# Four heads and both out-projections of the first mixer in one block, the second mixer's compression inside its in-projection

## What is computed

```python
# first mixer (mLSTM, 4 heads of 512), evaluated for all 512 tokens at once
x_in, z = jnp.split(h @ w_in, 2, axis=-1)
x_conv = silu(causal_conv4(x_in)); q, k, v = blockwise 4x4 products
s = (q k^T / sqrt(512)) * weights(i, f gates), causal
hh = s @ v / max(|s.sum(-1)|, floor); hn = layernorm(hh) * ln_w
x = x + ((hn + skip * x_conv) * silu(z)) @ w_out
# second mixer (nsa_mixer), 16 query heads in 4 groups of head size 64
q, k_c, v_c, k_s, v_s, k_w, v_w, z, g_logit = split(h @ w_in)
k_cmp = silu(blocks of 32 tokens, stride 16, of k_c + pe, @ w1[0]) @ w2[0]   # v_cmp alike
p_cmp = masked_softmax(q k_cmp^T * scale)                                     # 31 columns a head
q_r, k_s, k_w = rope_partial(...)
o = gate0 * (p_cmp @ v_cmp) + gate1 * selected attention + gate2 * window attention
x = x + (o * silu(z)) @ w_out
```

## Time and profile before

| what | value |
|---|---|
| median of 3 runs | 2141.22 us (2139.99 to 2141.77) |
| the profiled execution | 2139.64 us, of which the span is 2137.9 us |
| mean granted TensorE clock | 0.946 |
| TensorE, Vector, Scalar busy | 91%, 53%, 32% of the span |
| HBM | 73 GB/s over the span |

### The profile page before, as it was taken

One profiled execution on the slowest core, in us unless ns is written; L12 is line 12 of the kernel. 1 busy time (PEld: TensorE's weight loads), 2 busy tenths in 40 slices (PEclk: granted clock), 3 DMA queues, 4 the chain that ended last, 5 costly groups with the idle time before them and its releaser, 6 DMA issues. The chain is left out here.

```text
span 2137.9 us, 35810 instructions
## 1 busy us (share of the span) xinstructions
PE 1948.5 (91%) x15360; PEld 1547.3 (72%) x15360; DVE 1130.4 (53%) x1696; ACT 692.6 (32%) x1137; POOL 150.1 (7%) x161
## 2 busy tenths in 40 slices
PE   8999987978999879989999984998889999999997
PEld 8676845647888656677887853887887788888875
DVE  3654344353433657854435785777747354454544
ACT  3224322122212247854221164433323322222242
POOL 1100011011000300002002001000000100000011
PEclk9999988979999869999999995999999999999998
DMA  4323421112423000012432010000103322323220
GB/s 150 103 90 104 148 79 50 69 49 84 174 99 123 6 20 12 11 60 84 151 121 79 30 43 1 3 3 4 63 22 141 107 99 95 103 82 103 76 94 40
DMA packets 40429, 158.91 MB, mean 74 GB/s; under 512 B 4304, under 2 KB 13008, under 8 KB 25680
## 3 DMA queue, kind: packets, MB, share of 16 engines
q1 hardware_dynamic: 26064, 141.94, 19.3%
q10 hardware_dynamic: 14208, 14.68, 1.9%
HBM read 139.83 MB, written 16.78 MB: 73 GB/s over the span
## 5 line engine op out<-in xcount | busy, mean ns | idle before, releaser
L239 PE MATMUL ps<-act_hi,whi 128*128 128x512 f32 x1408 | 565.0, 401 | 35.9 <-PEq L828 15.6
L240 PE MATMUL ps<-act_lo,whi 128*128 128x512 f32 x1408 | 555.3, 394 | 0.0
L241 PE MATMUL ps<-act_hi,wlo 128*128 128x512 f32 x1408 | 554.7, 394 | 0.0
L239 PEld LDWEIGHTS ps<-act_hi,whi 128*128 128x128 f32 x1408 | 268.8, 191 | 106.7 <-issue 46.5
L221 DVE TENSOR_TENSOR wlo<-raw,whi 128x2048 fp32r<-128x2048 f32 (+2 forms) x113 | 251.1, 2222 | 171.5 <-ACT whi L212 171.3
L212 ACT ACTIVATE whi<-raw 128x2048 fp32r<-128x2048 f32 (+2 forms) x113 | 209.1, 1851 | 360.8 <-PE ps L241 226.0
L240 PEld LDWEIGHTS ps<-act_lo,whi 128*128 128x128 f32 x1408 | 269.2, 191 | 57.8 <-issue 2.9
L241 PEld LDWEIGHTS ps<-act_hi,wlo 128*128 128x128 f32 x1408 | 268.7, 191 | 57.4
L2706 PE MATMUL ps<-f_hi,whi 128*128 128x512 f32 x256 | 99.6, 389 | 0.0
L2707 PE MATMUL ps<-f_lo,whi 128*128 128x512 f32 x256 | 99.6, 389 | 0.0
L2708 PE MATMUL ps<-f_hi,wlo 128*128 128x512 f32 x256 | 99.6, 389 | 0.0
(11 more groups left out here) (448 smaller groups left out, 2908.2 us busy)
## 6 DMA issues: line engine op xcount, KB each, us to landing
raw<-stream_in SPq DMA_DIRECT2D x107, 1024.0 KB, 4.9
v_scratch<-v_out ACTq DMA_DIRECT2D x16, 256.0 KB, 2.5
z_scratch<-zt ACTq DMA_DIRECT2D x16, 256.0 KB, 2.9
ml_v<-v_scratch SPq DMA_DIRECT2D x4, 1024.0 KB, 4.9
ml_z<-z_scratch SPq DMA_DIRECT2D x16, 256.0 KB, 2.6
cmp_w<-cmp_w_in SPq DMA_DIRECT2D x2, 2048.0 KB, 9.6
z_scratch<-in_zt ACTq DMA_DIRECT2D x16, 256.0 KB, 2.0
mix_g<-z_scratch SPq DMA_DIRECT2D x16, 256.0 KB, 6.3
```

What stands on the lines that cost most here:

```text
L239: pe.matmul(bank, hi, k.act_hi[:, kt, :], start=(kt == 0), stop=False)
L240: pe.matmul(bank, hi, k.act_lo[:, kt, :], start=False, stop=False)
L241: last = pe.matmul(bank, lo, k.act_hi[:, kt, :], start=False, stop=(kt == rows // P - 1))
```

## The change

The heads of the first mixer and its two out-projections become one stage. PE's list there: while head h is finished (outputs, transposes `turned`), the key products and scores of head h+1 stand between. They use banks 4 and 5 alone; the normalised head has a buffer of its own (`hn`), and its transposes go to banks 0 to 3. After heads 1 and 3 follow the eight tiles of an out-projection (`product`): four tiles over the older head's y, then the same four over the younger's, then the other four whole, in banks 4 to 7 and 0 to 3. After head 3 its own transposes stand between the two halves.

In the second mixer the gate tile moves ahead of the z tiles, and `stage_nsa_prep` and `stage_nsa_cmp` vanish as stages: their work follows single tiles of the in-projection (tiles 12 to 28) in the same stage. The rotation works in place on `k.q`. In the attention the transposed scores `pt` lie in two weight buffers, and one wait goes.

```diff
-    cols("nsa_in", 0, D, 0, 29 * P)
+    cols("nsa_in", 0, D, 0, 20 * P)
+    cols("nsa_in", 0, D, 28 * P, 29 * P)
+    cols("nsa_in", 0, D, 20 * P, 28 * P)
...
+            values(0)
+            gate(0, 0)
+            gate(0, 1)
+            for h in range(ML_HEADS):
+                if h < LAST:
+                    values(h + 1)
+                gate(h, 2)
+                gate(h, 3)
+                if h < LAST:
+                    gate(h + 1, 0)
+                    gate(h + 1, 1)
+                if h % 2:
+                    load_blocks(k, sp, out0 + 4 * (h // 2) + 4 + RAW_SLOTS)
...
+            def selected(h):
+                if h:
+                    pe.wait_ge(s["wexp_raw"], TT * h)
...
+            def keys(h):
                 for c in range(TT):
...
+                    t = TT * h + c
+                    if c < 2 and h:
+                        pe.wait_ge(s["st_done"], TT * h)
+                    if c < 2 and h == LAST:
+                        pe.wait_ge(k.evac_done, added(1, 1))
+                    if c >= 2:
+                        pe.wait_ge(s[("k_act", "k_dve")[c % 2]], 2 * h + 1)
+                    pe.matmul(k.ps[:, 4 + c % 2, :], k.qk[:, t, :], k.xconv[:, t, :], start=True, stop=True) \
+                        .then_inc(s["k_mm"], 1)
+
+            def scores(h, j):
+                pe.wait_ge(s["k_act"], 2 * h + 2)
+                pe.wait_ge(s["k_dve"], 2 * h + 2)
+                if j >= 2:
+                    pe.wait_ge(s["st_done"], TT * h + j - 1)
+                for c in range(TT):
+                    last = pe.matmul(k.ps[:, 4 + j % 2, j * P:S], kk[:, c, j * P:(j + 1) * P],
+                                     k.xconv[:, TT * h + c, j * P:S], start=(c == 0), stop=(c == TT - 1))
...
+            def outputs(h):
                 pe.wait_ge(s["v_landed"], 16 * (h + 1))
                 for i in range(TT):
                     pe.wait_ge(s["st_done"], TT * h + i + 1)
+                    if h:
+                        pe.wait_ge(s["y_read"], TT * (h - 1) + i + 1)
+                        pe.wait_ge(s["r2v_done"], h)
+                    if h == 2:
...
+            def product(h, n, kts):
+                b, j = adds(h)[n]
+                pe.wait_ge(k.lo_done, b + 1)
+                w0 = BLOCKS[b][4]
+                for kt in kts:
+                    if n == 0:
+                        pe.wait_ge(s["y_lo"], TT * h if kt < TT else TT * h + kt - TT + 1)
+                    w = slice(kt * w0 + j * P, kt * w0 + j * P + P)
+                    hi, lo = k.whi[b % 2][:, w], k.wlo[b % 2][:, w]
+                    bank = k.ps[:, add_bank(n), :]
+                    pe.matmul(bank, hi, k.act_hi[:, kt, :], start=(kt == 0), stop=False)
+                    pe.matmul(bank, hi, k.act_lo[:, kt, :], start=False, stop=False)
+                    last = pe.matmul(bank, lo, k.act_hi[:, kt, :], start=False, stop=(kt == KD - 1))
+                if kt == KD - 1:
+                    last.then_inc(k.tile_done, 1)
...
+
+            selected(0)
+            keys(0)
+            for j in range(TT):
+                scores(0, j)
+            for h in range(ML_HEADS):
+                if h < LAST:
+                    selected(h + 1)
+                outputs(h)
+                if h < LAST:
+                    keys(h + 1)
+                    scores(h + 1, 0)
+                    turned(h, 0)
+                    turned(h, 1)
+                    scores(h + 1, 1)
+                    turned(h, 2)
+                    turned(h, 3)
+                    scores(h + 1, 2)
+                    scores(h + 1, 3)
+                if h % 2:
+                    ahead = h + 1 if h < LAST else h
+                    pe.wait_ge(s["st_done"], TT * (ahead + 1))
+                    pe.wait_ge(s["wexp_raw"], TT * (ahead + 1))
+                    for n in range(4):
+                        if n == 3:
+                            pe.wait_ge(s["r2v_done"], h + 1)
+                        product(h, n, range(TT))
+                    if h == LAST:
+                        for c in range(TT):
+                            turned(h, c)
+                    for n in range(4):
+                        product(h, n, range(TT, KD))
+                    for n in range(4, KD):
+                        pe.wait_ge(s["y_read"], TT * (h + 1))
+                        product(h, n, range(KD))
...
+            for h in range(ML_HEADS):
+                ahead = h < LAST
+                if ahead:
+                    weights(h + 1, 0)
+                    weights(h + 1, 1)
+                    keys(h + 1, 0)
+                root(h)
+                if ahead:
+                    keys(h + 1, 2)
+                normed(h)
+                if ahead:
+                    weights(h + 1, 2)
+                high(h, 0)
+                if ahead:
+                    weights(h + 1, 3)
+                for c in range(1, TT):
+                    high(h, c)
+                if h % 2:
+                    b = out0 + 4 * (h // 2)
+                    for n in range(KD):
...
+            for h in range(ML_HEADS):
+                ahead = h < LAST
+                statistics(h)
+                if ahead:
+                    keys(h + 1, 1)
+                scales(h)
+                if ahead:
+                    keys(h + 1, 3)
+                normed(h)
...
-                    dve.tensor_tensor(y[:, c % 2, :], y[:, c % 2, :], z[:, c % 2, :], ALU.mult).then_inc(s["y_done"], 1)
+                    if ahead:
+                        weighted(h + 1, c)
...
+                if n < 4:
+                    evicted(pe, (12, 13, 16, 17)[n])
+                if n == 0:
+                    pe.wait_ge(s["hid_done"], 1)
+                elif n <= 4:
+                    pe.wait_ge(s["rot_read"], n)
+                elif n == 5:
+                    pe.wait_ge(s["p_ready"], 3)
+                else:
+                    pe.wait_ge(s["rot_read"], n - 1)
+                pe.matmul(k.ps[:, rot_bank(n), :], k.const("rot"), src[:, i, :], start=True, stop=True) \
+                    .then_inc(s["rot_mm"], 1)
...
+            for t, (b, j) in enumerate(tiles):
                 multiply_tile(k, pe, b, j, norm if t == 0 else None)
                 if t == 0:
                     norm.last_mean(pe)
                 if t == 1:
                     norm.spread(pe)
+                if 12 <= t < 20:
+                    for x in range(8):
+                        hidden((t - 12) // 4, 8 * ((t - 12) % 4) + x)
+                if 17 <= t < 21:
+                    value(t - 17)
+                if t in (17, 18, 20):
+                    turn((17, 18, 20).index(t))
+                if t == 20:
+                    compressed()
+                if t == 21:
+                    turn(3)
+                    gates()
+                if 21 <= t < 25:
+                    scores(t - 21)
+                if 23 <= t < 27:
+                    probabilities(t - 23)
+                if t >= 25:
+                    turn(2 * t - 46)
+                    turn(2 * t - 45)
+
...
+                if t >= Z0:
+                    evicted(act, t)
+                    z = t - Z0
+                    act.activation(zt[:, z % 2, :], zt[:, z % 2, :], ACT.Silu).then_inc(z_ready, 1)
+                    act.wait_ge(z_ready, z + 1)
+                    act.dma_start(k.io["z_scratch"][z], zt[:, z % 2, :]).then_inc(stored[z % 2], 16)
...
+                if t == 21:
+                    rope(3)
+                if 21 <= t < 25:
+                    subtract_top(t - 21)
+                if 22 <= t < 26:
+                    weigh(t - 22)
+                if 23 <= t < 27:
+                    probabilities(t - 23)
+                if t >= 25:
+                    rope(2 * t - 46)
+                    rope(2 * t - 45)
+
...
-    p = k.region("att_p", [P, 3, 2, S], F32, 0)
-    pt = k.region("att_pt", [P, 4, 2, S], F32, 12)
+    p = k.region("att_p", [P, 3, 2, S], F32, 16)
+    pt = [k.at(f"att_pt{i}", [P, 2, 2, S], F32, at) for i, at in enumerate((84, 100))]
...
-                act.wait_ge(s["sc_mm"], 32 * (gp + 1))
...
-        lambda k: stage_ml_heads(k, 0),
-        lambda k: stage_add(k, out0, out0 + 4),
-        lambda k: stage_ml_heads(k, 2),
-        lambda k: stage_add(k, out0 + 4, out0 + 8, norm_nsa),
+        lambda k: stage_ml_heads(k, norm_nsa),
         lambda k: stage_nsa_in(k, norm_nsa),
-        stage_nsa_prep,
-        stage_nsa_cmp,
         stage_nsa_attention,
```

More of the change, by code:

```diff
@@ L1010, in _ @@
             for x in range(2):
[L1011 to L1029 removed]
+                pool.memset(k.taps[x][:, :, S:S + CMP_BLOCK], 0.0).then_inc(s["cleared"], 1)
```

684 lines of the change are left out of this document (365 added, 319 removed).

## The result

The changed kernel took 2065.24 us, the median of 2065.1, 2065.39, 2063.81 and 2072.97, against 2141.49 (4 runs) of the kernel before: a ratio of 0.9652, interval 0.9628 to 0.9677.

A forecast was written before the change was run, and what follows sets the result against it. TensorE, busy 91% of the span, was taken as the bound, leaving only its idle and half-clock time to win. 2139.64 - 39.4 (heads block) - 24.5 (in-projection) = 2075.7, or 2077.3 us as a median; range 2067 to 2101.

The forecast's parts named there:

- The attention begins at half clock now and will again: Start of the attention: 0.50 clock over 12.3 us stays; a gain of 2.8 counted in the range alone.
- Between heads: Three times in the head block, PE waits 0.4 and 0.8 on key copies: 1.2 each, 3.7 in all.
- Before the first out-projection: PE waits 2.6 for head 2's last weighted scores, then half clock loses 3.4: 6.0 in sum.
- Last y chain: Before the last out-projection's second half, PE waits on head 3's y chain: 7.6 idle, 3.0 at half clock.
- Block in all: Heads and out-projections to the next norm: 222.3 us in place of 261.75, saving 39.4.
- Compressed scores: Inside in-projection tiles, one row block's scores take 1.97 us at full clock, against 3.94 at half.
- The chain behind two tiles: In the in-projection, a block's softmax chain, pitch 8.1, is hidden behind two tiles of 14 us or more.
- End of the in-projection: After the last z tile, PE idles 3.3 us for Vector's eviction and rotations, ACT's gate and the store.
- the rival: In-projection: Vector and GpSimd wait for each other's whole steps, 1.26 more per weight split beside one; 2082 us, chance 6%.
- The stretch: The in-projection with the compression in it: 209.8 us in place of 234.3, saving 24.5.
- 1.6 to get from a profile to a median: Whole kernel: the profiled execution of 2139.64 was 1.6 below the median of 2141.22, so 2075.7 became 2077.3.

The follow-up runs named there:

- turn earlier: The changed kernel with the last head's y tiles turned after two of the four first halves of the out-projection, not all four: 2063.87 us, ratio 0.9636.
- probabilities one tile earlier: The changed kernel with PE's transposes of the compressed attention's probabilities in tiles 22 to 25 in place of 23 to 26: 2095.62 us, ratio 0.9794.
- heads only: The kernel before with the new four-head stage in place of its four stages, second mixer unchanged: 2096.86 us, ratio 0.9806.
- the second profile: The changed kernel run again with no edit; the profiled execution took 2077.11 us.

## Why the prediction was right and where it failed

The change was right in its mechanism, and the forecast was 12.1 us too slow, with the result 1.8 below the range. Two terms failed, both prices for half clock behind a pause: "I take the half clock, 3.4 lost" before the first out-projection, where the profile of the result shows none (block 3.4 shorter than forecast), and "The attention begins at half clock now and will again", at no gain, where 3.4 us at half clock came in place of 12.3 (3.7 less from there on). Term by term:

- **Between heads** (1.2 each): right. Waits of 0.88, a head's cycle of 332.29 - 304.84 = 27.45 where I had 27.2.
- **Before the first out-projection** (wait 2.6, then half clock, 3.4 lost; sum 6.0): the wait was sized right, 2.31. The half clock failed: the clock stayed at 1.00 in the profile of the result. In the other profiles with this pause it fell in five (three of the kernel after, *turn earlier*, *probabilities one tile earlier*), for 3.4 us and thus 1.7 lost, and stayed in one (*heads only*). It cost 0 or 1.7, and never 3.4.
- **Last y chain** (7.6 idle, 3.0 at half clock; 10.6): waits of 5.8, and 10.2 us at 0.52, part of it in those waits. From the first product of the last half at 432.08 to the end of the out-projection at 487.86 PE takes 55.8 for 45.7 of work (87.1 / 2 and 2.2): 10.1 lost. That is right in the sum, in part by luck: PE idled 1.8 less than forecast and lost more at half clock (10.1 - 5.8 = 4.3 for 3.0).
- **Block in all**: 222.3 forecast, 218.94 measured, 3.4 off; 221.39 in the second profile, 0.9 off.
- **Compressed scores** (1.97 at full clock, 3.94 at half): right, at full clock, 1.93 from a block's mask product at 640.56 to the next tile at 642.49. **The chain behind two tiles**: right, with 3.84 of slack (ready at 653.66, turned at 657.50), and *probabilities one tile earlier* shows that in this order of Vector's it needs both.
- **End of the in-projection** (3.3 idle): 2.24. Vector's last two sums take 0.69 each, with no product of GpSimd beside them; the first of the two:

```profile
695.55 0.69 DVE L1431 TENSOR_TENSOR nsa_q<-nsa_turned,nsa_straight 128x512 f32<-128x512 f32 x1
```

  GpSimd's last product ended at 692.33, so these two did not meet one. In the tiles ahead they did. Two rows of GpSimd, and the two of Vector beside them:

```profile
676.15 1.29 POOL L1253 TENSOR_TENSOR nsa_straight<-nsa_q,consts 128x512 f32<-128x512 f32 x1 [32.02 <-DVE nsa_q L1431]
...
683.84 3.26 POOL L1253 TENSOR_TENSOR nsa_straight<-nsa_q,consts 128x512 f32<-128x512 f32 x1 [0.62 <-DVE nsa_q L1431]
```

```profile
676.71 1.28 DVE L1431 TENSOR_TENSOR nsa_q<-nsa_turned,nsa_straight 128x512 f32<-128x512 f32 x1
...
683.69 2.28 DVE L223 TENSOR_TENSOR wlo<-raw,whi 128x2048 fp32r<-128x2048 f32 x1
```

  The sum at 676.71 began 0.56 after GpSimd's product and ended 0.55 after the product's end; it took 1.28 where 0.69 is its time alone. The product at 683.84 began 0.15 after Vector's weight split, which took its usual 2.28, and itself took 3.26 in place of 1.29. In both pairs the second to start did little or nothing until the first had ended. That is the rule of the Trainium skill (SBUF — State Buffer, section "SBUF: two separate sides"), that of GpSimd and a Vector step with two inputs in SBUF the one that starts first holds the shared ports for its whole instruction and the other fully blocks, and here the trace agrees. The 0.57 of the earlier trace rows, which I read as bearing it out in part only, is the same case: that sum, too, began 0.56 into the product beside it. What the rival had wrong is the price. It added a whole step of 1.26 to every weight split, but a split that starts first isn't held up, and a sum waits only for the rest of a product, the 0.57 already counted. Tiles 25 to 28 have a pitch of 7.2 to 7.6 and no such wait of PE. The stretch was 209.8 forecast, 207.35 and 206.26 measured.
- **The attention** ("begins at half clock now and will again"): wrong by size. It has 3.4 us at half clock, not 12.3; I had 2.8 for it in the range alone, and this stretch and all behind it took 3.7 less. The start of it, with the same matmuls, in the kernel before, in heads only and in the kernel after:

```profile
768.70:808.70 40.00, 36.87 (x307) 23.84 (x308) 26.53 (x66) 27.12 (x80) 0.00 (x0) 0.84 0.09 28
```

```profile
725.49:763.13 37.64, 33.55 (x307) 22.50 (x308) 26.50 (x66) 27.11 (x80) 0.00 (x0) 0.95 0.09 29
```

```profile
697.89:735.41 37.52, 33.44 (x307) 22.47 (x308) 26.53 (x66) 28.37 (x81) 0.00 (x0) 0.95 0.10 29
```

  So 2.4 to 2.5 of the 3.7 are gained in these 40 us. They aren't owed to the compression's new place: heads only, which has the compressed attention of before as a stage of its own right ahead of it, gains 2.4 there as well. What ends the half clock earlier is not settled. The rest of the 3.7 comes and goes: in the second profile half clock elsewhere makes the whole stretch 3.5 longer than before (1372.75 against 1369.2), so the 3.7 are not a sure gain.

The 12.1 between 2077.3 and 2065.24 are 3.4 of the block, 2.4 of the in-projection (1.1 of it the wait at its end), 3.7 from the attention on, 1.1 ahead of the block, and 1.4 because I added 1.6 to get from a profile to a median, where 0.1 was right, to the rounding. The orders, waits and their places were right; mis-sized was the half clock that follows a pause, in the two terms above. I took the trace of before as if its half clock belonged to its pauses by a fixed price. The low end of the range allowed for it, but for nothing in the in-projection or in unchanged code, and so missed by 1.8.

Over the 16 executions of the kernel after the median is 2073.0, 4.3 below the forecast and inside the range. Three of the four recorded executions had the low level, and nothing here foretells which one a set of four shows: that the result fell outside the range is in part that draw. What decides the level is not settled. The pauses of PE don't show it: where I compared them (up to the block, the block with the in-projection, and the stretch from 860) the same ones stand in high and low profiles, with sums a row that differ by up to 0.7 us either way. Nor does the clock behind the pause of 2.31: it fell in a profile of the low level too (2067.05). I can't say either whether the kernel before has levels that lie closer together, or none.

## What to carry to other kernels

Work of the next unit placed between the dependent steps of this one is worth the waits and the half clock behind them: here 48.7 us of block for the same instructions in another order, 18.3 of them waits that the old order has only because the keys now share two banks. So when an experiment takes back an order, look for waits that the test itself brings in before it is read as the worth of the rest. Count how many tiles of distance a chain needs in the queues of all its engines, since one too few on PE gives nearly all back (22.5 of 26.9). When gains get down to a few waits of 2 us, compare stage lengths of profiles beside whole times, and run the unchanged kernel in every set: here its medians went from 2065.24 to 2074.60.

## What was not expected of the hardware

- The same pause of 2.31 us is followed by full clock in two profiles and by 3.4 us of half clock in five; after pauses of 3.64 and 6.27 there were 6.8 us at half clock, in one profile each.
- A half-clock stretch that lies partly in the pause costs only what is left of it, as far as one profile of each shows: 4.0 more of pause made the block 2.9 to 5.4 longer, and 1.3 more made it 1.9 to 4.3 longer.
- One program, one chip: executions of 2064.9 and 2077.1 us. Between the profiles of 2065.1 and 2077.1, 7.2 us lie from the attention on and 3.4 ahead of the block.
- Vector's sum of two SBUF tiles beside GpSimd's product ended 0.55 after it (1.28 in place of 0.69), and GpSimd's product that began 0.15 after Vector's weight split took 3.26 in place of 1.29: the later of the two waits for the earlier.
